# The output gate's projection moves from the front stage into the mLSTM steps, and two modulation groups move to the first output projection

## The reference, cut to what matters

```
mods = silu(c) @ ada_w[l] + ada_b[l]                 # 6 vectors of 1024 for each of 2 layers, 9 rows of c
h = x * (1 + scale1) + shift1
q, k, v, o, gates = split(h @ w_in)                  # 512, 512, 1024, 1024 and 16 columns
hh = mlstm_chunkwise(q, k, v, gates)                 # a recurrence over chunks of tokens
y = (norm(hh) * norm_g * sigmoid(o)) @ w_out         # o is the output gate
x = layer_norm(ALPHA * x + gate1 * y)
```

## Time and profile before

| what | value |
|---|---|
| median of 3 runs | 2689.26 us |
| lowest and highest | 2684.11 and 2690.96 us |
| span of the profiled execution (first to last instruction) | 2673.1 us |
| median less span, what lies around it | 16.2 us |
| TensorE busy | 2371.8 us, 89% of the span |
| VectorE busy | 1380.5 us, 52% |
| ScalarE busy | 1048.6 us, 39% |
| GpSimd busy | 320.0 us, 12% |
| mean granted clock of TensorE | 0.919 |

### The profile page before, as it was taken

One profiled execution on the slowest core, in us unless ns is written; L12 is line 12 of the kernel. 1 busy time (PEld: TensorE's weight loads), 2 busy tenths in 40 slices (PEclk: granted clock), 3 DMA queues, 4 the chain that ended last, 5 costly groups with the idle time before them and its releaser, 6 DMA issues. The chain is left out here.

```text
span 2673.1 us, 40044 instructions
## 1 busy us (share of the span) xinstructions
PE 2371.8 (89%) x11761; PEld 1766.1 (66%) x11761; DVE 1380.5 (52%) x2288; ACT 1048.6 (39%) x1771; POOL 320.0 (12%) x394
## 2 busy tenths in 40 slices
PE   2999999787949999999598999999989589999976
PEld 0876666565837788788387666666668477788851
DVE  2412310456876655656384343434458766655657
ACT  1211120533125654655242334343431246654645
POOL 1000000551001100110010223100000011100103
PEclk7899999777969999999798999999999789999985
DMA  6156653745136866876644545323241368866856
GB/s 264 48 183 216 216 200 126 222 142 194 40 123 239 311 243 220 309 263 212 199 155 155 164 138 179 110 90 102 95 168 55 123 216 297 305 226 235 302 195 221
DMA packets 193772, 501.45 MB, mean 188 GB/s; under 512 B 19364, under 2 KB 39301, under 8 KB 187176
## 3 DMA queue, kind: packets, MB, share of 16 engines
q1 hardware_dynamic: 165080, 404.85, 44.4%
q0 software_dynamic: 19056, 66.20, 7.0%
q10 hardware_dynamic: 9536, 29.13, 2.9%
HBM read 434.51 MB, written 68.77 MB: 188 GB/s over the span
## 5 line engine op out<-in xcount | busy, mean ns | idle before, releaser
L1818 DVE TENSOR_TENSOR e_wl<-e_raw,e_wh 128x1024 fp32r<-128x1024 f32 x384 | 449.2, 1220 | 96.4 <-ACT e_wh L1729 96.1
L1729 ACT CAST e_wh<-e_raw 128x1024 fp32r<-128x1024 f32 x384 | 382.2, 1048 | 99.3 <-DMA e_raw<-in_e_up 42.3
L1648 PE MATMUL e_psG<-e_wh,e_xh 128*128 128x512 f32 x784 | 322.2, 411 | 10.2 <-issue 7.4
L1650 PE MATMUL e_psG<-e_wh,e_xl 128*128 128x512 f32 x784 | 312.3, 398 | 0.0
L1649 PE MATMUL e_psG<-e_wl,e_xh 128*128 128x512 f32 x784 | 310.9, 397 | 0.0
L1648 PE MATMUL e_psY<-e_wh,e_hh 128*128 128x512 f32 x392 | 159.6, 407 | 24.7 <-DVE e_hl L1841 24.7
L519 PE MATMUL in_ps<-in_w_upper,in_h_upper 128*128 128x512 f32 (+1 forms) x432 | 178.3, 413 | 0.0
L1648 PEld LDWEIGHTS e_psG<-e_wh,e_xh 128*128 128x128 f32 x784 | 149.2, 190 | 42.8 <-issue 8.3
L1650 PEld LDWEIGHTS e_psG<-e_wh,e_xl 128*128 128x128 f32 x784 | 148.7, 190 | 37.2
L520 PE MATMUL in_ps<-in_w_lower,in_h_upper 128*128 128x512 f32 (+1 forms) x432 | 172.5, 399 | 0.0
L521 PE MATMUL in_ps<-in_w_upper,in_h_lower 128*128 128x512 f32 (+1 forms) x432 | 171.8, 398 | 0.0
(11 more groups left out here) (538 smaller groups left out, 4393.0 us busy)
## 6 DMA issues: line engine op xcount, KB each, us to landing
e_raw<-in_e_gate SPq DMA_DIRECT2D x32, 2048.0 KB
e_raw<-in_e_up SPq DMA_DIRECT2D x32, 2048.0 KB
e_raw<-in_e_down SPq DMA_DIRECT2D x32, 2048.0 KB
x<-in_ada_w SPq DMA_DIRECT2D x40, 1024.0 KB, 5.3
yrows<-e_y ACTq DMA_DIRECT2D x49, 512.0 KB, 7.8
x<-in_cache SPq DMA_DIRECT2D x64, 320.0 KB, 3.4
a_pages<-in_cache SPq DMA_DIRECT2D x64, 320.0 KB, 3.4
in_w_raw<-in_a_w_in POOLq DMA_DIRECT2D x48, 256.0 KB, 4.4
```

Of the source, the lines that this page charges most:

```text
L1648: T.matmul(out, upper[:, k, :], wh[:, z, cols], start=k == 0, stop=False)
L1650: mm = T.matmul(out, lower[:, k, :], wh[:, z, cols], start=False, stop=k == PIECES * n - 1)
L1729: S.copy(wh[:, z, c * PC:(c + 1) * PC], raw[:, z, c * PC:(c + 1) * PC]).then_inc(s_hi[z], 1)
L1818: V.tensor_tensor(wl[:, z, at], raw[:, z, at], wh[:, z, at].bitcast(F32), ALU.subtract).then_inc(s_lo[z], 1)
```

## The change

1. The front stage has four chunks (q, k, v) in place of six and computes the modulation groups 1 to 3 there. It stores `qkv` in whole tiles of 128 rows, and it also stores the transposed rows h, upper and lower part, in the DRAM tensor `hT`, 1 MB a tile. It prepares the weights of columns 2048 to 2559 for the next stage. The small vector work moves to earlier chunks.
2. In the mLSTM stage a tile's output gate is computed a step ahead by `gate(i, a)`, a = 0 and 1, with 24 matmuls each. Both share the bank `psY` with `turn_y`, in the order of the list TURNS. `hidden` loads h, `open_gate` on ScalarE takes the bank out with a Sigmoid. The weights of the last 512 columns are loaded and split at the stage's beginning. `keep_y` writes to a small buffer, which ScalarE's own DMA queue stores in the DRAM tensor `mixD`.
3. The first output projection loads its rows from `mixD`, and its loop has the 16 pieces of groups 4 and 5, loaded on GpSimd's queue and taken out by ScalarE.

```diff
@@ stage_front
-    CHUNKS = A_IN // HALF
-    PIECE = 4 * HALF
+    CHUNKS = QKV // HALF          # 4
+    PIECE = ADA_PIECE
-        GROUPS_AFTER = CHUNKS - 1
+        GROUPS_AFTER = ADA_FRONT - 1
+                    if c == 0:
+                        for j, part in enumerate((hh[:, t, :, :], hl[:, t, :, :] if t < PT else hlS[:])):
+                            sp.dma_start(g.hT[t, :, j, :], part.rearrange("p k n -> p (k n)").bitcast(F32)
+                                         ).then_inc(s_hst, 16)
-                nc.scalar.activation(out[0:n, slot, :], ps[0:n, slot, :],
-                                     ACT.Sigmoid if c >= 4 else ACT.Copy).then_inc(s_ev, 1)
+                nc.scalar.copy(out[:, slot, :], ps[:, slot, :]).then_inc(s_ev, 1)
@@ stage_mlstm, tensor
+            def gate(i, a):
+                s, n = i % 2, bank_turn("gate", i, a)
+                pe.wait_ge(s_h[s], turn_no(i))
+                if n >= 1:
+                    pe.wait_ge(s_Yc, n)
+                out = psY[:].rearrange("p k n -> p (k n)")
+                for k in range(KD):
+                    if (i, a) == (0, 1):
+                        pe.wait_ge(s_lo, k + 1)
+                    T.matmul(out, ring[:, s, 0, k, :], g.w_upper[:, a, k, :], start=(k == 0), stop=False)
+                    T.matmul(out, ring[:, s, 0, k, :], g.w_lower[:, a, k, :], start=False, stop=False)
+                    mm = T.matmul(out, ring[:, s, 1, k, :], g.w_upper[:, a, k, :], start=False, stop=(k == KD - 1))
+                mm.then_inc(s_Y, 1)
+            gate(0, 0)
             turn(0)
+            gate(0, 1)
             scores(0)
             for i in range(LAST + 1):
                 if i != S:
                     add(i)
                 if i < LAST:
                     turn(i + 1)
+                if i >= 2:
+                    turn_y(i - 2, 0)
+                if i < LAST:
+                    gate(i + 1, 0)
                 products(i)
                 if sample_part(i) is not None:
                     add_sample(i)
                 if i < LAST:
                     scores(i + 1)
                 if i + 1 == S:
                     turn_by_batch()
                 if i >= 2:
-                    turn_y(i - 2, 0)
                     turn_y(i - 2, 1)
+                if i < LAST:
+                    gate(i + 1, 1)
@@ stage_mlstm, scalar
+            def open_gate(i, a):
+                act.wait_ge(s_Y, bank_turn("gate", i, a) + 1)
+                if i >= 2:
+                    act.wait_ge(s_sga, i - 1)
+                A.activation(sig[:, i % 2, a * HALF:(a + 1) * HALF], psY[:].rearrange("p k n -> p (k n)"), ACT.Sigmoid)
+                act.drain()
+                act.sem_inc(s_Yc, 1)
+                act.sem_inc(s_sig, 1)
             for i in range(LAST + 1):
                 if i < LAST:
                     queries_keys(i + 1)
+                if i >= 2:
+                    keep_y(i - 2, 0)
                 if i + 1 == S:
                     by_batch()
+                if i < LAST:
+                    open_gate(i + 1, 0)
                 if sample_part(i) is not None:
                     decay(i)
                 keep(i)
                 ...
                 if i + 2 <= LAST:
                     exponentials(i + 2)
                 if i >= 2:
-                    keep_y(i - 2, 0)
                     keep_y(i - 2, 1)
+                if i < LAST:
+                    open_gate(i + 1, 1)
@@ stage_out_proj, tensor
             for t in range(TILES - 2):
+                left = iter(range(pieces_before(t), pieces_before(t + 1)))   # 0, 2, 3, 3, 2, 3, 3 pieces
                 project(t + 2, range(KD // 2))
                 turn(t)
-                project(t + 2, range(KD // 2, KD))
+                for piece in islice(left, 1):
+                    ada_piece(piece)
+                project(t + 2, range(KD // 2, 3 * KD // 4))
+                for piece in islice(left, 1):
+                    ada_piece(piece)
+                project(t + 2, range(3 * KD // 4, KD))
                 logits(t)
+                for piece in left:
+                    ada_piece(piece)
@@ stage_out_proj, scalar
             for t in range(TILES):
+                if done < GROUPS_LEFT and pieces_before(t - 1) >= KD * (done + 1):
+                    group_out(done)
+                    done += 1
```

More of the change, by code:

```diff
@@ L1 @@
 from contextlib import ExitStack
+from itertools import islice
 import math
@@ L312, in _ @@
             modulate(PT, NSAMP, 1)
+            nc.vector.memset(hlS[:].bitcast(F32), 0.0)
+            v.drain()
             lower(v, 1, PT // 2 - 1, 1)
@@ L796, in _ @@
             for i in range(2, LAST + 1):
+                hidden(i)
                 if i < LAST:
@@ L805, in _ @@
             sp.wait_ge(s_st, 32)
-        def loads(i):
-            return turn_no(i) + (48 if i >= S and i % 2 == S % 2 else 0)
+            for z in range(2):
+                sp.wait_ge(s_mix[z], 16 * TILES)
         @block.tensor
@@ L942, in _ @@
             G = nc.gpsimd
+            for k in range(KD):
+                po.dma_start(land[k], g.a_w_in[k * P:(k + 1) * P, A_IN - HALF:A_IN]).then_inc(s_w[k], 16)
             po.wait_ge(s_set, 1)
@@ L1092, in decay @@
                 c.then_inc(s_dec, 1)
+            exponentials(0)
+            upper(0)
+            upper(1)
             queries_keys(0)
-            exponentials(0)
+            for k in range(2, 5):
+                upper(k)
+            open_gate(0, 0)
+            for k in range(5, KD):
+                upper(k)
+            open_gate(0, 1)
             act.wait_ge(s_zero, 1)
@@ L1295, in _, with ada_piece @@
             T = nc.tensor
+            def ada_piece(piece):
+                j, k, r = piece // KD, piece % KD, piece % RING
+                pe.wait_ge(s_aw[r], 16 * (piece // RING) + 16)
+                if k == 0 and j >= 1:
+                    pe.wait_ge(s_ae, j)
+                for q in range(4):
+                    mm = T.matmul(psA[32 * q:32 * q + 9, :], g.silu[:, k * 9:(k + 1) * 9],
+                                  ada[:, r, q * HALF:(q + 1) * HALF], start=(k == 0), stop=False)
+                mm.then_inc(s_ap, 1)
+                if k == KD - 1:
+                    pe.wait_ge(s_ab, 64 * j + 64)
+                    for q in range(4):
+                        mm = T.matmul(psA[32 * q:32 * q + 9, :], g.ones[32 * q:32 * q + 1, 0:9], ab[32 * q:32 * q + 1, :],
+                                      start=False, stop=True)
+                    mm.then_inc(s_am, 1)
             def project(t, ks):
```

320 lines of the change are left out of this document (220 added, 100 removed).

## The result

The changed kernel took 2702.16 us (median of 5 runs, 2698.45 to 2711.87). The kernel before, in the same runs, took 2689.26. The ratio is 1.0065, with a 95% interval of 1.0046 to 1.0083: slower, as forecast (2705). Timed again in 6 runs beside 17 of the kernel before, it took 2702.98 against 2683.57, ratio 1.0075 (1.0059 to 1.009).

A forecast was written before the change was run, and what follows sets the result against it. TensorE was taken to bound the front and output projection; the mLSTM stage had idle time and a slow clock. −119.2 + 37.5 + 72.7 + 2.9 + 21.7 = +15.6 on 2689.3 gave about 2705, range 2672 to 2724.

The forecast's parts named there:

- Front: Front stage: two ordinary chunks of 59.6 us each go, since TensorE is the only bound; −119.2 us.
- Start of the mLSTM stage: mLSTM stage, first load to end of step 1: 37.5 us more, of which 32.7 are six half gates.
- Steps 2 to 7: mLSTM stage: gate matmuls, two new bank waits, semaphores and slow clock lengthen these steps from 95.4 to 168.1 us, +72.7.
- the clock: mLSTM steps 2 to 6: half rate loses 2.6 us in each of steps 2 to 5, 1.5 in step 6; 12.
- The waits: Shared bank, mLSTM stage: first gate half waits 1.3 us; second 1.0 in steps 2 to 5, 3.85 in step 6.
- the slow clock stays as it is: Rival, mLSTM steps: slow clock costs 27 us in place of 12; time 2720, chance 0.15.
- the clock holds: Rival, mLSTM stage: dense gate matmuls keep full clock, so the 12 us go; time 2689, chance 0.2.
- End: End of the mLSTM stage: last store of mixed rows must land, 2.4 us, and ScalarE's DMA issues cost 0.5; +2.9.
- Projection: First output projection: +1 at the start, 18.7 for pieces and bias on TensorE, +2 in the tail; +21.7 us.
- The sum: Whole kernel: all stage terms together give +15.6 us, added to 2689.3 for 2704.9.
- only TensorE's content: Rival, mLSTM steps take only TensorE's work: 2670, chance 0.23; needs second bank wait under 1 us, full clock, growth under 97.5.
- the second bank wait: mLSTM stage: gate(i+1,1) waits for keep_y(i-2,1), 1.0 us in steps 2 to 5, 3.85 in step 6, 0.8 in step 7.

The follow-up runs named there:

- e8: Changed kernel with psY's users served earlier in the mLSTM stage and modulation group 5's copy moved in the projection: 2679.67 us, ratio 0.9979 to the kernel before.
- b1: Kernel before, with both turn_y calls and both keep_y copies moved earlier in its mLSTM stage: 2718.99 us, ratio 1.0124 to the kernel before.
- e12: e8 with the next tile's first gate half split around products and the second turn_y behind add_sample: 2677.88 us, ratio 0.9987 to the kernel before.
- b2: Kernel before with only ScalarE's order changed, both keep_y copies ahead of the exponentials: 2685.11 us, ratio 1.0004 to the kernel before.

## Why the prediction was right

The side was right, and so was the time, 2702 for 2705, though its closeness is partly luck (see the sum). The mechanism was right as well: no single bound, but 24 us of projection which nothing hides and an mLSTM stage that takes back all that the front gives. Point by point:

- **Front, −119.2 forecast, −115.9 measured.** Missed by 3.3. I had taken every chunk for an ordinary one of 59.6. Before, chunks 1 to 5 took 63.6, 59.8, 59.6, 63.3 and 59.6; now chunks 1 to 3 take 67.5, 60.0 and 61.8. So the last three became one, for 120.7, which is more than forecast, and chunk 1 took back 3.9. There TensorE waited 2.70 for the first piece of `ada_w` (0.28 before), whose load was asked for at 161.29, behind the last stores of h (159.60 before), and then ran at 1.2 GHz (clock 0.50 from 170 to 172). Chunk 0 took 0.9 more. I had given SyncE's 18 stores no price; that they caused the wait fits these rows, but no run took them away.
- **Start of the mLSTM stage, +37.5; measured +34.1** (+33.6 by the means). h came in 4.9 where I had 7, but the second half waited 5.18 for the split weights.
- **Steps 2 to 7, +72.7; measured +80.1.** This is the term that was mis-sized, and in it the clock: 12 forecast. In step 5 half rate cost 0.7 in `add_sample`, 0.9 in scores, 0.45 in `turn_y` and 2.05 in the gate half, 4.1 in all, where I took 2.6; steps 3 and 4 are like it, step 2 lost 2.7, and step 6 lost 2.8 in the gate half alone, where I took 1.5. That makes some 18. The gate's pitch of 0.2345 for 0.227 is 2.2 more. The waits were close: 1.59, 0.79 and 3.87 for 1.3, 1.0 and 3.85. The rival "the slow clock stays as it is" (27) was too high, "the clock holds" (0) wrong. I had also misread the slow stretch of the earlier trace rows, 568 to 577: it holds only the last 0.2 us of `add_sample`, and what runs at half rate in it is scores, `turn_y` and the next `add`:

```profile
565.34 2.89 PE L864 MATMUL m_psU<-m_va,x 16*128 16x129 f32 x16
568.30 2.08 PE L829 MATMUL m_psT<-m_qT,m_kT 64*128 64x128 f32 x16
```

- **End, +2.9; measured +1.9. Projection, +21.7; measured +23.2** (+24.4 by the means): +2.7 at the start, +19.6 in the loop (18.7 forecast), +0.9 in the tail, where I had 2.
- **The sum** was +15.6. The same terms measured +23.4 in the first profiles and +23.8 by the means, so it was 8 us too low; the time itself rose by 12.9 in the first runs and by 19.4 in the larger set. I let 16.2 us stand between the span and the median of before, as if they lay around it. There is no such thing around the span: a run's time is 1.6 or 1.7 above its own span (2702.16 and 2700.5 after, 2687.31 and 2685.7 in the second profile before). The other 14.5 was run-to-run scatter. Added to the first profile alone the sum gives 2690.4, 12 below the measured time, of which 8 are the terms and 4 the rest of the program. That the forecast came within 3 us is owed to that scatter.
- **The rival "only TensorE's content"** (2670) failed where I said it would be decided: the second bank wait was under 1 us in five steps of six, but the clock was not full (mean 0.83 in steps 3 to 5), and the stage grew by 116, not by less than 97.5. Its place was right, though. With the bank's users reordered (e8) the stage grows by 93.4 over the mean of before, and the time is under the kernel before.

## What to carry over

Work moved into a stage with idle time and a low clock does not come free: ask for each instruction queued behind a shared PSUM bank which copy frees it, and put the bank's users ahead of long ScalarE work before judging the move; here that order, with one copy moved in the projection, was worth some 23 us, more than the 19.4 that the move cost. The best order depends on the length of the step, so one that repairs the long step can break the short one (41.9 us of waits in b1). Before adding a term to one profile's span, take a second profile: the untouched stages behind the projection moved by 10 us between two.

## What was not expected of the hardware

- The clock fell to 0.50 with TensorE 91% busy (e8, step 4, 9.06 us of the stretch from 495 to 505) and no idle gap over 0.4 us in that stretch; small matmuls in a row were enough. With twelve dense ones set between them (e12) it stayed at 1.00 in steps 3 and 5, where e8 had 0.87, and still fell in steps 2 and 4. The Trainium skill's page "TensorE: Matmul & The Clock Gate", "HAM oscillation — how this bites in real kernels", ties such falls to idle gaps; this trace shows one without.
- The same three matmuls of 512 columns take 0.227 each in the front and 0.2345 in the mLSTM stage, both at clock 1.00. I did not find out why.
- The start of the old mLSTM stage took 35.5, 37.8 and 42.2 in three profiles of the same instructions (the third is b2, whose edit begins at step 2). The clock goes with it: 0.92 from 485 to 490 in the first, and 0.50 from the first load to 497 in the third.
